# Two mixers of a three-layer block: other places in the queues for rotary sums, the gates' logarithm, normed heads and output triples

## The reference

```python
proj = rmsnorm(h) @ w_in                       # q, k, v of 8 gated and 4 differential heads, gates
log_f = log_sigmoid(ff + forget_bias); cum_f = cumsum(log_f)
q_d, k_d = rope(dq), rope(dk)                  # rotary, differential heads only
p = softmax(q k^T * scale (+ cum_q - cum_k), causal)
a_d = p_d[:, 0] - lam * p_d[:, 1];  o_d = rmsnorm(a_d @ v_d) * (1 - lambda_init)
o_f = p_f @ v_f
x = x + concat(o_f, o_d) @ w_out
```

## Time and profile before

| | |
|---|---|
| device time, median of 3 runs | 2735.28 us (2734.5 to 2742.32) |
| profiled execution: its own time | 2743.0 us |
| its span | 2741.2 us |
| TensorE busy | 2688.1 us, 98% |
| VectorE busy | 1392.7 us, 51% |
| ScalarE busy | 1001.6 us, 37% |
| GpSimd busy | 183.9 us, 7% |
| steps 0 to 31 of the first mixer | 419.1 to 634 us |
| steps 0 to 31 of the second mixer | 1429.1 to 1640 us |

### The profile page before, as it was taken

One profiled execution on the slowest core, in us unless ns is written; L12 is line 12 of the kernel. 1 busy time (PEld: TensorE's weight loads), 2 busy tenths in 40 slices (PEclk: granted clock), 3 DMA queues, 4 the chain that ended last, 5 costly groups with the idle time before them and its releaser, 6 DMA issues.

```text
span 2741.2 us, 33940 instructions
## 1 busy us (share of the span) xinstructions
PE 2688.1 (98%) x12772; PEld 2202.0 (80%) x12772; DVE 1392.7 (51%) x1937; ACT 1001.6 (37%) x1560; POOL 183.9 (7%) x142
## 2 busy tenths in 40 slices
PE   7999998999999999999998999999999999999999
PEld 6888886787888888888876878888887888788887
DVE  5444256665544326444267665444235557844443
ACT  4222134454322224222144444223235453334553
POOL 1000022201000001000042101000000000010000
PEclk9999999999999999999999999999999999999999
DMA  3222232111222222222232112222222222322111
GB/s 142 100 92 99 94 106 70 62 54 70 100 92 99 97 87 100 99 97 94 100 100 77 49 37 100 97 95 99 92 92 70 77 85 81 107 93 93 62 62 66
DMA packets 70326, 239.18 MB, mean 87 GB/s; under 512 B 8528, under 2 KB 10832, under 8 KB 70224
## 3 DMA queue, kind: packets, MB, share of 16 engines
q1 hardware_dynamic: 69936, 237.00, 25.7%
q10 hardware_dynamic: 288, 0.79, 0.1%
HBM read 230.15 MB, written 2.10 MB: 85 GB/s over the span
## 4 chain that ended last, share of the span: by engine, by line
PE 88%; DVE 5%; DMA 2%; ACT 1%; POOL 1%; DVEq 1%; issue 1%; SPq 1%; ACTq 0%; POOLq 0%
PE bank L391 20%; PE bank L393 19%; PE bank L392 19%; PE score L391 5%; PE score L392 5%; PE score L393 5%; PE flip_bank L391 2%; PE flip_bank L393 2%; PE flip_bank L392 2%; PE score L1067 1%; DMA tmp<-tmp 1%; DVE w_lo L374 1%; SPq L453 1%; PE flip_bank L1089 1%; DVE rstd L386 1%
## 5 line engine op out<-in xcount | busy, mean ns | idle before, releaser
L374 DVE TENSOR_TENSOR w_lo<-w_raw,w_hi 128x1024 fp32r<-128x1024 f32 x427 | 525.0, 1231 | 546.7 <-ACT w_hi L334 533.9
L391 PE MATMUL bank<-h_hi,w_hi 128*128 128x512 f32 x1896 | 762.9, 402 | 15.9 <-DVE w_lo L374 8.6
L393 PE MATMUL bank<-h_hi,w_lo 128*128 128x512 f32 x1896 | 743.6, 392 | 0.0
L392 PE MATMUL bank<-h_lo,w_hi 128*128 128x512 f32 x1896 | 743.1, 392 | 0.0
L334 ACT ACTIVATE w_hi<-w_raw 128x1024 fp32r<-128x1024 f32 x427 | 447.6, 1051 | 408.0 <-DMA w_raw<-stream 407.5
L391 PEld LDWEIGHTS bank<-h_hi,w_hi 128*128 128x128 f32 x1896 | 359.5, 190 | 94.8 <-issue 14.3
L393 PEld LDWEIGHTS bank<-h_hi,w_lo 128*128 128x128 f32 x1896 | 358.8, 189 | 77.1
L392 PEld LDWEIGHTS bank<-h_lo,w_hi 128*128 128x128 f32 x1896 | 359.8, 190 | 73.1 <-issue 2.6
L531 ACT ACTIVATE hid_hi<-tmp 128x512 f32 (+1 forms) x88 | 55.6, 632 | 410.4 <-DVE tmp L709 410.4
L703 DVE TENSOR_TENSOR tmp<-bank,rstd 128x512 f32<-128x512 f32 x132 | 91.2, 691 | 146.1 <-PE bank L393 146.1
L526 ACT ACTIVATE tmp<-tmp 128x512 f32<-128x512 f32 x88 | 55.6, 632 | 249.2 <-DVE tmp L703 249.2
(11 more groups left out here) (486 smaller groups left out, 3877.1 us busy)
## 6 DMA issues: line engine op xcount, KB each, us to landing
w_raw<-stream SPq DMA_DIRECT2D x427, 512.0 KB, 3.3
tmp<-tmp SPq DMA_DIRECT2D x64, 64.0 KB, 2.0
x_tok<-x SPq DMA_DIRECT2D x4, 512.0 KB, 6.3
wx_raw<-stream SPq DMA_DIRECT2D x4, 512.0 KB, 4.4
out<-out_tok SPq DMA_DIRECT2D x8, 256.0 KB, 2.0
tmp<-qr SPq DMA_DIRECT2D x16, 64.0 KB, 2.2
tab_in_f<-tables SPq DMA_DIRECT2D x1, 704.0 KB, 8.6
cos_sin<-rope ACTq DMA_DIRECT2D x1, 512.0 KB, 4.4
```

Source lines behind the costliest of these rows:

```text
L374: nc.vector.tensor_tensor(w_lo[:, s, :], w_raw[:, s, :], w_hi[:, s, :].bitcast(F32), ALU.subtract).then_inc(lo_ready, 1)
L391: nc.tensor.matmul(dst, whi, xhi, start=start, stop=False)
L392: nc.tensor.matmul(dst, whi, xlo, start=False, stop=False)
L393: return nc.tensor.matmul(dst, wlo, xhi, start=False, stop=stop)
```

## The change

The diff has five parts, alike in both mixers.

- VectorE: in a step, `rope_add` now comes after evacuations, cuts, weighing, gates' work and `v_low`, and those of q and k of pair 1 move from the units ahead into steps 0 and 1. `diff_low` comes right behind the weighing. From step 28 (`PACED`) on the cuts come behind both.
- ScalarE: `v_high` and plain halves come ahead of the rotated halves; those of pair 1 move into steps 0 and 1 too; from step 28 on the cuts come behind the exponentials.
- The gates' logarithm goes from step 4 to the end of step 5, and VectorE's sums and parts of the gates start a step later (6 and 7 to 9, before 5 and 6 to 8).
- The copy of a normed head into `o_hi` goes from its own step to the next, behind the exponentials.
- PE: three output triples of m = 3 are made before the last triples of m = 0 to 2, step 31 has four early triples instead of six, and four stand ahead of `flip` of step 31.

```diff
--- before.py
+++ after.py
@@ -275,7 +275,8 @@
         GATES_AT = 3
 
         OUT_EARLY = [(m, kt) for m in range(3) for kt in (4, 5, 6, 7, 0, 1)] + [(m, 2) for m in range(3)]
-        OUT_CUT = (0, 3, 6, 9, 15, 19, 21)
+        OUT_EARLY += [(3, kt) for kt in (4, 5, 6)]
+        OUT_CUT = (0, 3, 6, 9, 13, 17, 21, 24)
 
 
         def in_unit(kind, g):
@@ -548,11 +549,13 @@
                     act_root(r)
 
             def mixer(layer, r, n0):
-                def gates():
+                def gates_exp():
                     act.wait_ge(g_step, 2 * layer + 1)
                     nc.scalar.activation(gate_rows[:, 1, :], gate_rows[:, 0, :], ACT.Abs)
                     act.drain()
                     nc.scalar.activation(gate_rows[:, 1, :], gate_rows[:, 1, :], ACT.Exp, scale=-1.0)
+
+                def gates_log():
                     act.drain()
                     nc.scalar.activation(gate_rows[:, 1, :], gate_rows[:, 1, :], ACT.Ln,
                                          bias=1.0).then_inc(g_step, 1)
@@ -620,28 +623,38 @@
                     act_cut(n0 + i + 2)
                     if i == 5:
                         v_high(0)
-                    kind, g = MIX_ORDER[i - 2] if i >= 2 else ("", 0)
-                    if kind in ("q", "k"):
-                        high_half(kind, g)
-                high_half("k", 1)
+                    if i in (2, 3):
+                        high_half(*MIX_ORDER[i - 2])
                 for k in range(NSTEP + 1):
                     g, b = k // TB, k % TB
-                    for i in CUTS_AT[k]:
-                        act_cut(n0 + i)
+                    if k < PACED:
+                        for i in CUTS_AT[k]:
+                            act_cut(n0 + i)
                     if k >= 2:
                         flip_high(k - 2)
                     if k < NSTEP:
                         exps(k)
+                    h = spread_at(k - 1)
+                    if h is not None:
+                        act.wait_ge(d_norm, DIFF_HEADS * layer + h + 1)
+                        nc.scalar.activation(o_hi[:, 4 + h, :], d_raw[:, h, :], ACT.Copy).then_inc(od_half, 1)
+                    if k >= PACED:
+                        for i in CUTS_AT[k]:
+                            act_cut(n0 + i)
+                    for _, h in units_at(k - 1, "v") if k else []:
+                        v_high(h)
+                    for kind, h in units_at(k, "qk"):
+                        if not is_diff(h):
+                            high_half(kind, h)
+                    if k < 2:
+                        high_half("qk"[k], 1)
                     for kind, h in units_at(k - 1, "qk") if k else []:
                         if is_diff(h):
                             high_half(kind, h)
-                    for kind, h in units_at(k, "qk"):
-                        if not is_diff(h):
-                            high_half(kind, h)
-                    for _, h in units_at(k - 1, "v") if k else []:
-                        v_high(h)
                     if k == GATES_AT + 1:
-                        gates()
+                        gates_exp()
+                    if k == GATES_AT + 2:
+                        gates_log()
                     if b == 2 and 1 <= g <= DIFF_HEADS:
                         act.wait_ge(d_out, DIFF_HEADS * layer + g)
                         nc.scalar.activation(d_squares[:, g - 1, :], d_raw[:, g - 1, :], ACT.Square).then_inc(d_sq, 1)
@@ -651,10 +664,6 @@
                         act.wait_ge(d_stat_in, DIFF_HEADS * (layer + 1))
                         nc.scalar.activation(d_stat[:, :], d_stat[:, :], ACT.Sqrt, scale=1.0 / P,
                                              bias=small[:, 0:1]).then_inc(d_root, 1)
-                    h = spread_at(k)
-                    if h is not None:
-                        act.wait_ge(d_norm, DIFF_HEADS * layer + h + 1)
-                        nc.scalar.activation(o_hi[:, 4 + h, :], d_raw[:, h, :], ACT.Copy).then_inc(od_half, 1)
                 flip_high(NSTEP - 1)
                 pair_high(GROUPS - DIFF_HEADS - 1)
                 for m in range(KT):
@@ -843,30 +852,38 @@
                     if i == 5:
                         v_low(0)
                     evacuate(i)
-                    kind, g = MIX_ORDER[i - 1] if i else ("", 0)
-                    if kind in ("q", "k"):
-                        rope_add(kind, g)
+                    if i in (1, 2):
+                        rope_add(*MIX_ORDER[i - 1])
                 for k in range(NSTEP + 1):
                     g, b = k // TB, k % TB
                     if k < NSTEP:
                         maxima(k)
                     if k >= 2:
                         flip_low(k - 2)
+                    for i in EVACS_AT[k]:
+                        evacuate(i)
+                    if k < PACED:
+                        for i in CUTS_AT[k]:
+                            dve_cut(n0 + i)
+                    if k < NSTEP:
+                        weigh(k)
+                    h = spread_at(k - 1)
+                    if h is not None:
+                        diff_low(h)
+                    if k >= PACED:
+                        for i in CUTS_AT[k]:
+                            dve_cut(n0 + i)
+                    if k == GATES_AT + 3:
+                        gates_sum()
+                    if 0 <= k - GATES_AT - 4 < len(CUM_ROWS):
+                        gates_part(k - GATES_AT - 4)
+                    for _, h in units_at(k - 1, "v") if k else []:
+                        v_low(h)
+                    if k < 2:
+                        rope_add("qk"[k], 1)
                     for kind, h in units_at(k - 1, "qk") if k else []:
                         if is_diff(h):
                             rope_add(kind, h)
-                    for i in EVACS_AT[k]:
-                        evacuate(i)
-                    for i in CUTS_AT[k]:
-                        dve_cut(n0 + i)
-                    if k < NSTEP:
-                        weigh(k)
-                    if k == GATES_AT + 2:
-                        gates_sum()
-                    if 0 <= k - GATES_AT - 3 < len(CUM_ROWS):
-                        gates_part(k - GATES_AT - 3)
-                    for _, h in units_at(k - 1, "v") if k else []:
-                        v_low(h)
                     if b == 1 and 1 <= g <= DIFF_HEADS:
                         dve.wait_ge(mixed, GROUPS * layer + g)
                         nc.vector.tensor_copy(d_raw[:, g - 1, :], bank[7][:, :]).then_inc(d_out, 1)
@@ -878,9 +895,6 @@
                     if (g, b) == (DIFF_HEADS + 1, 1):
                         dve.wait_ge(d_root, layer + 1)
                         nc.vector.reciprocal(d_stat[:, :], d_stat[:, :]).then_inc(d_inverse, 1)
-                    h = spread_at(k - 1)
-                    if h is not None:
-                        diff_low(h)
                     h = spread_at(k)
                     if h is not None:
                         dve.wait_ge(d_spread, DIFF_HEADS * layer + h + 1)
@@ -1041,8 +1055,10 @@
                             pe.wait_ge(lo_ready, n0 + MIX_IN + m + 1)
                             if m < 2:
                                 pe.wait_ge(in_evac, MIX_IN * layer + in_unit("qk"[m], GROUPS - 1) + 1)
+                            elif m == 2:
+                                pe.wait_ge(v_ready, GROUPS * (layer + 1))
                             else:
-                                pe.wait_ge(v_ready, GROUPS * (layer + 1))
+                                pe.wait_ge(exped, NSTEP * (layer + 1))
                         out_step(m, kt, kt == 4, False)
 
                 def turn_v(g):
@@ -1157,13 +1173,16 @@
                         diff_spread(spread_at(k))
                     for _, h in units_at(k, "v"):
                         turn_v(h)
+                out_early(4)
                 flip(NSTEP - 1)
-                out_early(4)
+                out_early(5)
                 mix(GROUPS - 1)
-                out_early(5)
+                out_early(6)
                 for m in range(3):
                     out_step(m, 3, False, True)
-                for m in range(3, KT):
+                for kt in (7, 0, 1, 2, 3):
+                    out_step(3, kt, False, kt == 3)
+                for m in range(4, KT):
                     pe.wait_ge(lo_ready, n0 + MIX_IN + m + 1)
                     for kt in (4, 5, 6, 7, 0, 1, 2, 3):
                         out_step(m, kt, kt == 4, kt == 3)
```

## The result

The changed kernel took 2710.48 us, median of 5 executions (2710.38 to 2712.31); the kernel before, measured with it (5 executions), 2735.96 (2734.5 to 2742.32). The ratio is 0.990, with an interval of 0.9889 to 0.9911: a gain of 1.0%. The forecast of 2703 was 7.5 us too low.

The account below looks back on a forecast made before the run. TensorE was taken as the bound, busy 2688.1 of 2741.2 us; 30.0 (idle) + 15.1 (clock) - 2 x 4.5 - 2 x 1.1 - about 0.4 = 33.5, less 1.5, gave 2735.3 - 32 = 2703 us, whole range 2693 to 2719.

Parts of the forecast that it names:

- The waits of today and their clock: In both mixers, TensorE loses 30.0 us to waits and 15.1 us to slow clock after them.
- Rotary sums last in the first steps: Steps 0 to 2: 8.2 us of waits and 2.0 of clock go, about 0.4 lost to a tight second step.
- Rival (c): First two steps: the wait moves from `v_lo` to the exponentials, 8.2 us and 2.0 of clock stay; 2713, chance 0.1.
- rival (a): Steps 6 to 12: nothing new waits and the clock never falls, so 9 us come back; 2694, chance 0.12.
- rival (d): Steps 8 and 12: rotated halves come too late for the scores, so slower; 2744 or more, chance 0.03.
- (e): No gain that shows: other waits of the same size take the places; chance 0.05.
- Steps 6 to 12: VectorE becomes an equal bound; new waits of 2.8 us plus 1.7 for contention, 4.5 us per mixer.
- Rival (b): Steps 6 to 12: VectorE is the bound, costing 17 us in place of 9; 2713, chance 0.2.
- the 5.2 worked out from it: Four VectorE-GpSimd exclusions per mixer, each about 1.3 us: 5.2 in place of 1.7, a sum 7 us smaller.
- The logarithm costed at nothing: Flip of step 4: about 1.2 us of wait goes per mixer; the moved load and logarithm (1.9 us) stay hidden.
- Normed heads and output triples: Per mixer, waits of 1.41 (step 27), 0.4 (`o_lo`) and 2.11 us (step 31) go; 1.1 new at m = 4.
- I take off 1.5: Cut from the 33.5 us sum, since the profiled execution's 7.7 us above the median may be clock time; 32 remain.

Follow-up runs that it names:

- u_rope: The changed kernel with rotary sums and rotated halves back where they stood, ahead of evacuations, cuts and weighing: 2725.86 us.
- y_gates_late: The changed kernel with VectorE's gates' sums moved to step 11 and their parts to steps 12 to 14: 2705.07 us.
- x_sum_later: The changed kernel with the gates' sums moved to step 7 and their parts to steps 8 to 10: 2714.82 us.
- u_gates: The changed kernel with the gates' logarithm and sums a step earlier again, as before the change: 2713.81 us.
- u_heads: The changed kernel with normed heads copied in their own step and the last steps' cuts and `diff_low` back: 2715.42 us.
- u_triples: The changed kernel with the order of the output triples as before the change: 2714.39 us.
- y_before: The kernel before, without an edit, run again for a second profiled execution: 2738.59 us, the profiled one 2736.47.
- best version: `y_gates_late` with two output triples of m = 3 taken forward in place of three: 2703.51 us.
- x_rope_only: The kernel before with only the changed order of rotary sums and rotated halves: 2722.26 us.

## Why the prediction was right, and where it was off

**The waits of today and their clock: right.** 45 us were lost in the two mixers, a third of it slow clock that shows as no wait. The clock's share was borne out: TensorE's busy time fell by 11.9 us with the same matmuls, 8.4 of them in the mixers by the stretches, and the first steps, without their waits, run at 1.00.

**Rotary sums last in the first steps: right in place and size.** Gain 10.2 us for 9.8. `v_lo` of pair 0 was ready 6 us ahead of the maxima in place of 5; step 1 has no wait, and one of 0.33 stands at the start of step 2 in the first mixer, against 0.4 allowed. `u_rope` shows that the gain is this part's. Rival (c), the wait moving to the exponentials, fell, as none above 0.33 is there; rival (a) fell by the new waits of steps 6 to 12; rival (d), as L1083 never waits for `k_lo`; and (e) by the time.

**Steps 6 to 12: right in kind, too small, and placed wrong.** The prediction put 1.4, 0.8 and 0.6 us at the flips of steps 6, 7 and 10, and 1.7 on contention, 9.0 in both mixers. Measured was a single wait, 2.95 and 2.61 us at the flip of step 6, and 3.3 and 3.4 of slow clock behind it, 12.3. The waits alone are what was reckoned without contention, 5.6 us in both mixers for 2 x 2.8; but they came as one wait in each, and the sum has no slow clock for it, as none followed waits of about a microsecond. Contention was counted as one cut slowed by 1.1 us; it reached three other instructions, 2.7 us longer in step 6 alone (the gates' sums, laid out with 1.9 us, took 3.0). Rival (b), VectorE as the bound at 17 us, is half right: what VectorE is given there does decide (`y_gates_late`, `x_sum_later`), but 12.3 is nearer to 9 than to 17, and its sign, more than 5 us of waits for `pt_lo` per mixer in steps 6 to 10, did not show.

The Trainium skill (SBUF — State Buffer, Who interferes with whom) says that GpSimd and VectorE can exclude each other for whole instructions. Durations of 1.21 to 1.77 against 0.48 to 0.67 agree in kind; with the 5.2 worked out from it the loss would have been 8 per mixer, where 6.3 and 6.0 were measured.

**The logarithm costed at nothing: right as far as it went.** The 1.2 us of step 4's flip became 0.34. Undone it costs 3.3 us, more than the 2 x 0.9 that its own wait lost, since that wait is 2.30 us in `u_gates`.

**Normed heads and output triples: right.** Steps 27 to 29 gained 3.9 for 3.6 (`u_heads` 4.9); `u_triples` has 3.9 for the triples, for 3.7, and the new wait at m = 4 is 1.18 and 0.94 us for 1.1.

**Where most of the error lies: from the profiled execution to the median.** The sum was made against an execution of 2743.0 us and gave 2709.5 for it, 1.1 us off. Then "I take off 1.5", and the 32 that were left were subtracted from the median of 2735.28, though the text itself said that the profiled execution stood 7.7 above it and that its extra might be clock time. An execution at the median had lost less, so it had less to win. `y_before` shows what lies between them: an execution 6.5 us shorter with nearly the same waits and 7.0 us less lost at the low clock. The kernel before scatters over 8 us, the changed one over 2. Of the error of 7.5 us, the sum's own is 1.1 and the rest comes from this step.

**Luck.** That the sum was off by only 1.1 us is in part luck. The table has steps 6 to 12 at 2.7 us less than forecast and the last row at 1.6 more, and 0.9 of that last row was won before the first mixer, by a clock that no part of the change touches.

What stays open: why the clock falls after a wait of 2.1 us once and not another time, and whether the best version's last wait goes with `v_low` ahead of the gates' part, and how much of the wait at the flip of step 6 would go if ScalarE made `pt_hi` ahead of the rotated half, the squares and the cut that stand before it in the chain above; no run has that order.

## What to carry to other kernels

Price a wait by what the clock does behind it as well: the waits of 2.95 and 2.61 us cost here more than twice what they showed, several of about a microsecond mostly only themselves. Subtract a gain from the very execution whose rows gave it, and look at the scatter of the others before moving it to a median; the kernels with many long waits scattered most here. In this stretch, where VectorE was nearly full, moving work within it moved the wait, and moving work out of it removed most of it. And an engine that idled beside another's work may find its instructions longer once it no longer idles: here VectorE's grew two- to threefold beside GpSimd's products.

## What was not expected of the hardware

The clock does not answer to a wait in the same way each time. I took the granted clock of the 4 us behind each wait of over 1 us in the mixers of all fourteen profiled executions, one of each kernel here and `y_before`: of 30 waits of 1.0 to 1.6 us one was followed by a clock below 1.00, of 22 of 1.7 to 2.4 us eleven, and of 23 of 2.5 to 4.8 us twenty-one. The same 2.11 us at the same place had 0.53 once and 1.00 once. The scatter seems to go with such waits, though no run tests it alone: the executions of the kernel before lie over 8 us and those of `u_rope` over 7 and those of `x_rope_only` over 6, each with five or more waits above 1.7 us in its trace; those of all other kernels here, with four at most, lie within 5.

And a VectorE instruction with a single tensor input, the weighing of 128x384, took 1.21 us beside GpSimd's products and 0.48 with fills in their place; with the fills the changed kernel is 10.1 us faster, though GpSimd is busy for only 7% of its time.
